# A mixture-of-experts block: the transfers of w_down issued by ScalarE on its own queue

## What is computed

```python
def moe_ffn(h, w_router, b_router, w_gate, b_gate, w_up, b_up, w_down, b_down):
    logits = hf @ w_router + b_router              # 256 tokens, 32 experts
    top_v, top_e = lax.top_k(logits, 4)            # four experts for each token
    top_w = jax.nn.softmax(top_v, axis=-1)
    ...                                            # rows of a block: the tokens of one expert
    g = xblk @ w_gate[e] + b_gate[e]
    u = xblk @ w_up[e] + b_up[e]
    g = jnp.minimum(g, 7.0)
    u = jnp.clip(u, -7.0, 7.0)
    a = (u + 1.0) * (g * jax.nn.sigmoid(1.702 * g))
    y = a @ w_down[e] + b_down[e]                  # added to the tokens, times top_w
```

## Time and profile before

| | |
|---|---|
| median of 3 runs | 1181.02 us (1180.81 to 1181.11) |
| profiled execution | 1180.81 us |
| its span | 1179.1 us |
| PE busy | 1119.2 us (95%) |
| ACT busy | 179.7 us (15%) |
| DMA | 441.69 MB, mean 375 GB/s |
| 4096 KB transfers | 74, of them 25 of down; 50 us from issue to landing |

### The profile page before, as it was taken

How to read it: one execution, slowest core, us unless ns; L and a number is a source line. 1 busy time by engine, 2 the same in 40 slices (tenths; PEclk the granted TensorE clock), 3 DMA queues, 4 the chain that set the end, 5 groups by cost and what they waited for, 6 DMA issues and landing times.

```text
span 1179.1 us, 13581 instructions
## 1 busy us (share of the span) xinstructions
PE 1119.2 (95%) x5309; PEld 528.9 (45%) x5309; DVE 326.2 (28%) x783; ACT 179.7 (15%) x350; POOL 29.8 (3%) x39
## 2 busy tenths in 40 slices
PE   6999999999999999999999999999999999999997
PEld 5888888864333333333333333333333333333332
DVE  2799974324111111111112111111111111111111
ACT  2111266132001101101011000011000000000011
POOL 2340000000000000000000000000000000000000
PEclk9999999999999999999999999999999999999999
DMA  9965426558999999999999999999999999999996
GB/s 281 348 185 165 142 105 250 215 219 327 421 425 427 434 432 430 431 431 434 432 430 431 432 432 430 434 434 428 432 434 431 430 434 431 431 431 434 432 424 258
DMA packets 53701, 441.69 MB, mean 375 GB/s; under 512 B 4135, under 2 KB 34089, under 8 KB 36520
## 3 DMA queue, kind: packets, MB, share of 16 engines
q1 hardware_dynamic: 51856, 439.89, 90.0%
q0 software_dynamic: 432, 0.95, 0.4%
q10 hardware_dynamic: 1384, 0.44, 0.2%
HBM read 440.08 MB, written 1.05 MB: 374 GB/s over the span
## 4 chain that ended last, share of the span: by engine, by line
PE 87%; DMA 9%; another core or an unknown queue 2%; DVE 1%; ACT 1%; issue 0%; SPq 0%; ACTq 0%; DVEq 0%
PE bank L1367 51%; PE bank L1136 17%; PE bank L1337 5%; PE bank L1322 4%; DMA arena<-in_w_up 4%; DMA arena<-in_w_down 4%; PE bank L1246 2%; PE bank L1401 2%; PE bank L1374 1%; PE bank L1329 1%; PE bank L1408 1%; DMA arena<-in_x 1%; PE bank L1159 1%; PE bank L1185 0%
## 5 line engine op out<-in xcount | busy, mean ns | idle before, releaser
L1367 PE MATMUL bank<-arena,x_columns 128*64 128x512 f32 x2080 | 468.3, 594 | 25.8 <-DMA arena<-in_w_up 24.1
L1367 PEld LDWEIGHTS bank<-arena,x_columns 128*64 128x64 f32 x2080 | 149.4, 137 | 299.8 <-issue 274.1
L1367 PE MATMUL bank<-arena,act_columns 128*64 128x512 f32 x992 | 219.1, 593 | 11.1 <-DMA arena<-in_w_down 11.1
L1136 PE MATMUL bank<-arena 128*128 128x256 f32 x928 | 205.9, 383 | 0.0
L1136 PEld LDWEIGHTS bank<-arena 128*128 128x128 f32 x928 | 177.2, 192 | 26.2 <-issue 1.7
L1367 PEld LDWEIGHTS bank<-arena,act_columns 128*64 128x64 f32 x992 | 76.2, 137 | 150.7 <-issue 150.7
L784 DVE SCALAR_TENSOR_TENSOR arena<-arena x240 | 97.1, 483 | 0.2
L1009 DVE TENSOR_SCALAR bias_selector<-ones_bf,expert_onehot 96x64 bf16<-96x64 bf16 x32 | 7.6, 237 | 272.3 <-PE bank L1329 272.3
L1023 DVE TENSOR_SCALAR gate_clipped<-bank 128x512 f32<-128x512 f32 x32 | 22.2, 692 | 208.7 <-PE bank L1367 208.7
L1027 DVE TENSOR_SCALAR hidden<-bank 128x512 f32<-128x512 f32 x32 | 22.1, 692 | 188.0 <-PE bank L1367 188.0
L1337 PE MATMUL bank<-y_block,scatter 64*128 64x512 f32 x248 | 61.5, 614 | 0.0
(11 more groups left out here) (185 smaller groups left out, 476.6 us busy)
## 6 DMA issues: line engine op xcount, KB each, us to landing
arena<-in_w_up SPq DMA_DIRECT2D x25, 4096.0 KB, 50.7
arena<-in_w_down SPq DMA_DIRECT2D x25, 4096.0 KB, 50.9
arena<-in_w_gate SPq DMA_DIRECT2D x24, 4096.0 KB, 49.7
arena<-in_w_in SPq DMA_DIRECT2D x21, 1024.0 KB, 11.9
arena<-in_w_gate SPq DMA_DIRECT2D x10, 2048.0 KB, 12.2
arena<-in_w_up SPq DMA_DIRECT2D x9, 2048.0 KB, 12.3
arena<-in_w_down SPq DMA_DIRECT2D x8, 2048.0 KB, 15.9
arena<-in_w_gate SPq DMA_DIRECT2D x12, 1024.0 KB, 7.7
```

What stands on the lines that cost most here:

```text
L1136: last = pe.matmul(bank[n % 3][:, j * T:(j + 1) * T], w[:, c, j * P:(j + 1) * P], src[:, c, :], start=(c == 0), stop=(c == C - 1))
L1367: last = pe.matmul(dst[h * CAP:(h + 1) * CAP, :], lhs(row), cols(rows[:, row, :], h), start=(row == 0), stop=(row == MROWS - 1))
```

## The change

The downs n = 10, 13, ..., 91 (28 of them, `ACT_DOWNS`; they are down 2 to down 29) are no longer issued by SP. ScalarE issues them in `moe_block`, one in each of the blocks 1 to 28, directly behind the copy of y: that copy has waited for the product with matrix n - 6, so the buffer is free. They are all loaded whole; of those that came in parts before, 10 had four, 13 and 16 had two. Downs 4, 7, 94 and 95, and all gates and ups, stay with SP, in their old order among themselves. ACT's loop over blocks is now two blocks long, since the buffer alternates.

```diff
+ACT_DOWNS = range(10, NM - 4, 3)
+for _n in ACT_DOWNS:
+    ROW_PARTS[_n] = [(0, MROWS)]
...
             for n in range(PAIRS, WHOLES[0]):
-                for lo, hi in parts_of(n):
-                    refill(n, lo, hi)
+                if n not in ACT_DOWNS:
+                    for lo, hi in parts_of(n):
+                        refill(n, lo, hi)
...
                     b, j = divmod(i + 1, 3)
-                    sp.wait_ge(piece_done, cycle * (PAIRS * EW) + (FRONT + EW * (i - PAIRS) + EW))
-                    load(i, 0, MROWS, rows_full[i, 0], cycle * ROUNDS + (b if j < 2 else b - 1), j)
+                    if j < 2:
+                        sp.wait_ge(piece_done, cycle * (PAIRS * EW) + (FRONT + EW * (i - PAIRS) + EW))
+                        load(i, 0, MROWS, rows_full[i, 0], cycle * ROUNDS + b, j)
...
+            def next_down(n, e):
+
+                src = t_in["w_down"].rearrange("e (p k) n -> e p (k n)", k=MROWS)[bass.ds(e, 1)].rearrange("a p n -> p (a n)")
+                act.dma_start(pairs[n % PAIRS], src).then_inc(rows_full[n % PAIRS, 0], 16)
...
                 if y_before:
                     copy_y(b * MPE + (FRONT - LEAD + MPE))
+                if refilled is not None:
+                    next_down(refilled, b + 1)
                 act.wait_ge(actT_done, b + 1)
...
-            with act.Fori(1, NE - 2) as b:
-                moe_block(b)
+            with act.Fori(0, len(ACT_DOWNS) // ROUNDS) as cycle:
+                for r in range(ROUNDS):
+                    moe_block(cycle * ROUNDS + (r + 1), refilled=ACT_DOWNS[r])
+            moe_block(NE - 3)
```

More of the change, by code:

```diff
@@ L674, in copy_y, with moe_block @@
                 act.activation(dst, src[:], ACT.Copy).then_inc(yb_out, 1)
-            def moe_block(b, then_gather=True, y_before=True, y_after=False, sw=swT, columns=actT):
+            def next_down(n, e):
+                src = t_in["w_down"].rearrange("e (p k) n -> e p (k n)", k=MROWS)[bass.ds(e, 1)].rearrange("a p n -> p (a n)")
+                act.dma_start(pairs[n % PAIRS], src).then_inc(rows_full[n % PAIRS, 0], 16)
+            def moe_block(b, then_gather=True, y_before=True, y_after=False, sw=swT, columns=actT, refilled=None):
                 act.wait_ge(gmin_ready, b + 1)
```

## The result

| | before | after |
|---|---|---|
| median of 4 runs each, in turn on one chip | 1180.91 us (1180.54 to 1181.11) | 1194.71 us (1193.39 to 1195.97) |
| profiled execution, its span | 1180.81, 1179.1 us | 1195.97, 1194.2 us |
| last gate product starts | 1137.01 us | 1152.89 us |

The ratio is 1.0114 with a 95% interval of 1.0102 to 1.0126: **13.8 us slower**. The forecast was 1192.0 (1180 to 1199), slower.

A forecast was written before the change was run, and what follows sets the result against it. The DMA engines bound the late rounds (29.14 us, three matrices). PE falls 13.7 us back, less 2.8 and 0.45 at the end, 10.5 later, taken as +11 on 1181: 1192 us, range 1180 to 1199.

The forecast's parts named there:

- the bound and the law: Late rounds stay 29.14 us, three matrices at 432 GB/s; PE stands 13.7 us further back for the same bytes, paid once.
- two queues share, up is late, down never: Late rounds: each ring gets half the rate, down lands about 20 us after issue, PE waits only for up, 2.8 us a round.
- The issue on ACT: Down's issue on ACT between two copies: costs nothing, comes 0.9 us later than SP's, with 1.7 us still free.
- D: The time at which a down product ends in a late round, 754.87 us in the kernel before; landings are counted from it.
- The end: After the last ACT down, one 26.33 us round gives back 2.81 us and 0.45 us of waits go: 10.5 us later.
- Parts ... taken as 0.: Matrices 10, 13, 16 loaded whole: a hole of 0 to 1 us at matrix 10 against small rate gains, -0.5 to +1.
- something else: Other causes, later, such as the granted clock not holding at 1.00 through a wait of up to 5.6 us; chance 0.03.
- The steady state x: Landing of up after D in late rounds, alternating about 13.46 between 10.65 and 16.2; loss 9.1 to 11.9 us.
- One order for all: Rival: engines serve transfers by issue time whatever the queue, down lands as before; 1181, 1180 to 1182 us; chance 0.12.
- more bytes: Rival: two rings close gaps within an engine; 434 GB/s gives back 4 us, with the old order 1177; chance 0.06.
- ACT's ring starved: Rival: SP's ring has clearly more than two thirds, down lands last and PE waits for it; 1207 to 1217 us; chance 0.05.
- ACT's ring first: Rival: down gets all the rate until landed, the end 15 us later, 1196; inside the forecast range, within its 0.74.

The follow-up runs named there:

- e4: Against the kernel after: ACT issues only the downs of matrices 19 to 64 (blocks 4 to 19), SP those after; 1181.28 us against 1181.36 of the kernel before.
- e6: Against the kernel after: ACT issues a single down, matrix 64 in block 19, SP all others; 1180.40 us against 1180.89 of the kernel before.
- e5: Against the kernel after: ACT issues a single down, the last, matrix 91 in block 28; 1190.27 us against 1181.36 of the kernel before.
- e2: The kernel before with matrices 10, 13 and 16 loaded whole, all still on SP's queue; 1183.65 us against 1181.36.
- e1: The kernel after, but ACT issues downs only from matrix 19 on; 10, 13, 16 from SP in parts; 1194.44 us against 1181.36 of the kernel before.
- e11: Kernel after with ACT's downs only from matrix 19 on, plus six added unused matmuls in each of blocks 17 to 28; 1193.26 us, 1.0097 of before.
- e3: Kernel after with ACT's downs only from matrix 19 on, each issued one block later; 1204.79 us against 1180.89 of the kernel before.
- e9: Kernel after with ACT's downs only from matrix 19 on, plus six added unused matmuls in each of blocks 7 to 28; 1195.16 us, 1.0119 of before.
- e10: The kernel before with six added unused matmuls in each of blocks 7 to 28; 1195.30 us, 1.0124 of before.
- e12: The kernel before with six added unused matmuls in each of blocks 17 to 28; 1181.73 us against 1181.42.

## Why the prediction was right, and where it was off

**Right: the bound and the law.** The late rounds stay as long as three matrices take at 432 GB/s. In the timeline of after PE's waits stand like this (four of the eight):

```profile
756.14 5.35 PE L1383 MATMUL bank<-arena,x_columns 128*64 128x512 f32 x16 [2.48 <-DMA arena<-in_w_up]
815.63 5.19 PE L1383 MATMUL bank<-arena,x_columns 128*64 128x512 f32 x16 [4.91 <-DMA arena<-in_w_up]
872.69 5.35 PE L1383 MATMUL bank<-arena,x_columns 128*64 128x512 f32 x16 [2.64 <-DMA arena<-in_w_up]
932.18 6.64 PE L1383 MATMUL bank<-arena,x_columns 128*64 128x512 f32 x16 [4.90 <-DMA arena<-in_w_up]
```

Here one wait in two rounds; from 815.63 to 932.18 four rounds take 116.55 us, four times 29.14. PE stands further back for the same bytes, and this is paid once. e4, e6 and e5 show it from three sides: middle, middle, end.

**Right: two queues share, up is late, down never.** Announced were half for each ring (54.1% and 45.7% while both work, so a little more than half for down), a landing about 20 us after issue (23.4), waits for up only (29.8 us in 15 rounds, 2.0 a round; announced 2.8 in the mean; the rest is in what the lower clock takes), mostly in turns of large and small. The first wait was announced near 560 to 600 us; it ended at 552.05 (timeline of after), 8 us ahead of that, and the next at 611.55:

```profile
552.05 5.35 PE L1383 MATMUL bank<-arena,x_columns 128*64 128x512 f32 x16 [2.11 <-DMA arena<-in_w_up]
```

On this place the Trainium skill, "DMA: Bandwidth & Descriptors", says in "Queues, rings and completion order" that each engine alternates, packet by packet, between rings with work. The trace agrees nearly by packets (128 against 124 from 777 to 795 us), by bytes not fully (4.19 against 3.54 MB). The same page's "Issuing engines are not separate DMA queues" says that several issuers share the same DMA engines and save only issue time. The rate agrees, 432 GB/s before and after; the end-to-end time does not: the order of landing changed and the kernel was 13.8 us slower.

**The issue on ACT: right that it is free, wrong when it comes.** As the prediction put it, ACT would issue 0.9 us after D. It issues at 773.91, 0.14 us after the copy of y began and before that copy had ended: the DMA instruction did not wait for the ACTIVATE ahead of it. That gained nothing: with D = 773.74 the bytes of down flow from 777.4 us, D + 3.7 (announced D + 3), since the first of them took 3.5 us and not 2. Down has all its bytes by 795, D + 21.3 (announced D + 22.4).

**The end.** The chain of waits of after from the last shared round (start us, us, what; it puts a product's start 0.07 us later than the timeline does):

```profile
1092.48 0.68 PE bank L1417 x4
...
1105.80 5.17 PE bank L1383 x16
...
1123.22 0.68 PE bank L1417 x4
...
1149.56 0.68 PE bank L1417 x4
...
1152.96 3.58 PE bank L1383 x16
```

and the same round's end before:

```profile
1104.54 0.68 PE bank L1401 x4
```

At 1123.22 PE is 18.7 us later than the 1104.54 of before; the next round is 26.34 us long (1149.56 - 1123.22) as announced, and gives 2.8 back. By the timeline the last gate starts at 1152.89, 15.9 later than 1137.01 (announced 1148, 11 later). No wait for the DMA follows, and with the 0.45 and 0.3 more at the tail 15.1 remain in this execution, 13.8 between the medians.

**The terms that were mis-sized.** The forecast was 2.8 us short of the medians, 4.1 of the profiled execution (15.1 against 11).

- *"Parts ... taken as 0."* This failed. The queue ran empty. The step said that the transfers ahead of matrix 10 would last until 330.5, worked out from a median landing time of 9.2 us of four parts, and so found a hole of at most 1 us. In after, where nothing of matrix 10 is issued before 328.81, the rate from 325 to 335 us in 40 slices, and what SP's queue still had from 326 to 328.5, show when they really ended:

```profile
GB/s 229 131 66 0 33 33 33 0 0 0 0 0 0 0 0 0 0 0 0 1049 524 262 131 131 0 0 262 1311 393 131 0 393 1180 524 0 0 524 1311 262 0
```

```profile
q1 hardware_dynamic: 4, 0.02, 2.4%
```

  The transfers ahead were over near 326, some five microseconds earlier than the step had them. The next bytes, near 329.8, are matrix 10's own; the share of 0.26 from 326 to 330 above is nearly all theirs. e2 measured this term alone: 2.3 us. It shows at the end too. The windows from 1160 to 1170 us, before and after:

```profile
1160.00:1170.00 10.00, 9.45 (x42) 3.11 (x44) 0.00 (x0) 0.84 (x2) 0.00 (x0) 1.00 0.54 220
```

```profile
1160.00:1170.00 10.00, 10.00 (x50) 3.38 (x48) 2.77 (x4) 1.91 (x2) 0.00 (x0) 1.00 0.86 357
```

  The DMA is done 0.32 x 10 = 3.2 us later; "the DMA's last bytes at the old time" was wrong by this. Not all of it is the hole: e1, without one, has a share of 0.66 in this window, 1.2 us later than before, and e11 0.61, 0.7 us; e2, with the hole alone, has 0.86, as after. (Of the 5.0 us of the hole 1.8 or more have come back on the way; 1 GB/s more over 800 us is as much, and the views do not resolve that.)
- *The clock, kept at 1.00 in the sum and named only among "something else".* After waits of 2.1 us and more it mostly fell. The wait of 4.92 us at 611.55 and the windows behind it:

```profile
611.55 6.53 PE L1383 MATMUL bank<-arena,x_columns 128*64 128x512 f32 x16 [4.92 <-DMA arena<-in_w_up]
```

```profile
611.50:618.30 6.80, 6.75 (x20) 2.11 (x22) 0.00 (x0) 0.00 (x0) 0.00 (x0) 0.57 1.02 439
618.30:621.90 3.60, 3.60 (x20) 1.12 (x16) 0.10 (x1) 0.00 (x0) 0.00 (x0) 1.00 1.01 437
```

  0.57 of 2.4 GHz in the mean is close to the lower level, 1.2 GHz; then 1.00 again. Most of these slow stretches only shorten the next wait. The last one, 5.17 us instead of 3.65 at 1105.80, has no wait behind it to hide in: 1.5 us.
- *The steady state x.* I took the upper half of 9.1 to 11.9. What is left at 1123.22 after these two terms is 18.7 - 3.2 - 1.5 = 14.0, a lag within the 12.3 to 15.1 given. e11 has the same remainder: its last shared down ends at 1121.14, 16.6 late; its clock took 5.35 - 3.65 = 1.7 there and its DMA ends 0.7 late, which leaves 14.2.

The three sum to 14.0 + 3.2 + 1.5 - 2.8 - 0.8 = 15.1. That is an account of one execution: 14.0 is what the other terms leave, and 0.8 is the 0.45 and the 0.3 at the tail, read off and not explained. **Open** is why removing the hole (e1) gave nothing where e2 says 2.3. The same account of e1's profiled execution would be 17.8 (1122.34 - 1104.54) - 1.2 - 3.0 = 13.6: the DMA is late by 2.0 less than in after, but its last slow stretch takes 6.63 us instead of 3.65, 3.0 more, where after's takes 1.5 more. e11, which has no hole and ends in after's phase, loses 11.8 instead of 13.8, about what e2 says. Both point to the hole's gain being hidden by where e1's last waits fall, but the intervals of e11 and after overlap and I have not forced a kernel into either phase: not shown.

**The rivals.** *One order for all* is excluded by the landing after 23.4 us, *more bytes* by 432 GB/s. *ACT's ring starved* and *ACT's ring first* (1196, the nearest in time) are both excluded by 54 and 46%; the time alone would not have told ACT first from the forecast. The wait that stands behind "slower", PE's for up, is the one I had named.

## What to carry to other kernels

- Where the DMA sets the pace, keep the large transfers in the order in which they are used, in one queue. A second queue that shares fairly moves no byte sooner in sum, but lets what is needed later overtake what is needed now.
- What counts at the end is how much lies in memory unused while the last compute still has to be done. An early disorder, or a wait of 10 us in the middle, can be free; the same instruction near the end costs nearly its whole transfer (8.9 of 9.71 us).
- A buffer that is refilled in parts lets the transfer follow the reader. Whole, it waits for the reader's end plus the time to the first bytes, and if nothing else is queued there, that is idle DMA time (e2: 2.3 us at the end).

## What the hardware showed that I had not expected

- **Clock after idling.** Behind waits for up of 2.1 us and more PE mostly took 5.0 to 6.6 us for work of 3.65 (granted clock 0.57, 0.58); behind the waits of before, at most 1.7 us, it never did. But one wait of 2.19 us (1076.58 above) was followed by 3.65, and in e3 two waits for down of 2.57 and 2.67 us were followed by full speed too (7.09 us for 32 matmuls).
- **A DMA instruction on ACT starts beside the ACTIVATE ahead of it** (773.91 against 773.77 + 0.60) and delays the next one by 0.01 us.
- **Two queues are not shared exactly in halves**: 54.1% for the new one, 45.7% for the other in the transfer shown; in eight others of after the new one has 53 to 57%.
- **A lower clock without a wait.** From 320 to 345 us the granted clock was 0.93 in after, e1, e2 and e4 to e9, and 1.00 in before, e3 and e10 to e12, with PE busy 25.00 of 25.00 us in all of them. It is not the edits: e5 and e6 have the instructions of before up to there. I did not find what brings it. Where matrix 10 comes in parts, the DMA moved 388 to 398 GB/s there at 0.93 and 420 to 422 at 1.00; whether that costs anything at the end is not shown.
